# First attention's running sums as rounded high and low products, 384 columns at once

## The reference, cut to what matters

```python
z = jnp.einsum('bhqd,bhkd->bhqk', qb, kp) * scale
log_keep = jnp.where(mask, jax.nn.log_sigmoid(-z), 0.0)
later = lax.cumsum(log_keep, axis=3, reverse=True) - log_keep
a = jnp.where(mask, jnp.exp(jax.nn.log_sigmoid(z) + later), 0.0)
outs.append(jnp.einsum('bhqk,bhkd->bhqd', a, vp))
```

## Time and profile before

| | |
|---|---|
| three runs, median (lowest to highest) | 1855.86 us (1853.26 to 1858.29) |
| the profiled execution's own time | 1856.47 us |
| its span, first to last instruction | 1855.2 us |
| busy: PE, DVE, ACT, POOL | 92%, 64%, 41%, 22% of the span |
| first attention with its projections | about 24 to 131 us of the span |

### The profile page before, as it was taken

How to read it: one execution, slowest core, us unless ns; L and a number is a source line. 1 busy time by engine, 2 the same in 40 slices (tenths; PEclk the granted TensorE clock), 3 DMA queues, 4 the chain that set the end, 5 groups by cost and what they waited for, 6 DMA issues and landing times.

```text
span 1855.2 us, 23146 instructions
## 1 busy us (share of the span) xinstructions
PE 1704.7 (92%) x9262; PEld 1297.9 (70%) x9262; DVE 1187.9 (64%) x2130; ACT 753.1 (41%) x1323; POOL 402.9 (22%) x340
## 2 busy tenths in 40 slices
PE   8999999999999999999999999987888777878888
PEld 7979988977799888989989989873333333323333
DVE  5776645756476548854352666779677766677855
ACT  4655534344355436774353655443122121122211
POOL 0220000000000000003011000335645544545551
PEclk9999999999999999989999999999979988898899
DMA  6335554544445553423231325699999999999997
GB/s 253 135 120 213 183 187 176 182 167 160 164 173 191 189 181 137 171 83 107 77 113 46 111 78 184 256 393 419 423 421 421 423 420 422 422 421 421 422 421 299
DMA packets 62955, 453.85 MB, mean 245 GB/s; under 512 B 7000, under 2 KB 7128, under 8 KB 8448
## 3 DMA queue, kind: packets, MB, share of 16 engines
q0 software_dynamic: 37152, 268.45, 35.0%
q1 hardware_dynamic: 25040, 178.27, 27.0%
q10 hardware_dynamic: 656, 5.66, 0.9%
HBM read 451.15 MB, written 1.05 MB: 244 GB/s over the span
## 4 chain that ended last, share of the span: by engine, by line
PE 26%; DMA 14%; DVE 5%; ACT 2%; POOL 2%; issue 1%; DVEq 0%; ACTq 0%; POOLq 0%
DMA uv_rows<-expert_uv,index 14%; PE banks L2529 12%; PE banks L624 3%; PE banks L626 3%; PE banks L625 3%; DVE uv_rows L2715 3%; POOL uv_rows L2745 1%; PE banks L2303 1%; ACT diag L2594 1%; PE banks L1972 1%; PE banks L1961 0%; PE banks L2474 0%; PE banks L1954 0%; PE banks L2289 0%; POOL weights_lo L619 0%
## 5 line engine op out<-in xcount | busy, mean ns | idle before, releaser
L2529 PE MATMUL banks<-uv_rows,diag 128*128 128x512 f32 x1024 | 503.6, 654 | 116.9 <-ACT diag L2594 116.8
L610 DVE TENSOR_TENSOR weights_lo<-weights,weights_hi 128x1024 fp32r<-128x1024 f32 x325 | 397.2, 1263 | 256.2 <-ACT weights_hi L601 256.2
L2529 PEld LDWEIGHTS banks<-uv_rows,diag 128*128 128x128 f32 x1024 | 212.5, 211 | 406.7 <-issue 268.9
L601 ACT ACTIVATE weights_hi<-weights 128x1024 fp32r<-128x1024 f32 x328 | 329.2, 1052 | 356.1 <-PE banks L626 342.6
L624 PE MATMUL banks<-x_hi,weights_hi 128*128 128x256 f32 (+1 forms) x1472 | 427.6, 290 | 3.3 <-POOL weights_lo L619 1.2
L626 PE MATMUL banks<-x_hi,weights_lo 128*128 128x256 f32 (+1 forms) x1472 | 420.5, 286 | 0.0
L625 PE MATMUL banks<-x_lo,weights_hi 128*128 128x256 f32 (+1 forms) x1472 | 420.4, 286 | 0.0
L2715 DVE CUSTOM_DVE_ANT_0 uv_rows<-uv_rows,tokens 128x1024 f32<-128x1024 f32 x256 | 305.4, 1224 | 148.5 <-DMA uv_rows<-expert_uv,index 148.5
L2745 POOL DMA_INDIRECT uv_rows<-expert_uv,index x254 | 317.0, 1248 | 307.9 <-PE banks L2529 259.6
L624 PEld LDWEIGHTS banks<-x_hi,weights_hi 128*128 128x128 f32 x1472 | 282.0, 192 | 10.3 <-issue 3.0
L626 PEld LDWEIGHTS banks<-x_hi,weights_lo 128*128 128x128 f32 x1472 | 282.0, 192 | 0.0
(11 more groups left out here) (382 smaller groups left out, 2085.2 us busy)
## 6 DMA issues: line engine op xcount, KB each, us to landing
weights<-weights SPq DMA_DIRECT2D x164, 1024.0 KB, 4.8
uv_rows<-weights SPq DMA_DIRECT2D x4, 1024.0 KB, 7.7
uv_rows<-expert_uv,index POOLq DMA_INDIRECT x254, 17.5
sb_first<-constants_first ACTq DMA_DIRECT2D x1, 1920.0 KB, 8.6
sb_always<-constants_always ACTq DMA_DIRECT2D x1, 1627.5 KB, 6.8
sb_peer<-constants_peer ACTq DMA_DIRECT2D x1, 1544.0 KB, 7.8
h<-x SPq DMA_DIRECT2D x1, 1024.0 KB, 5.8
out<-h SPq DMA_DIRECT2D x4, 256.0 KB, 4.5
```

Source lines behind the costliest of these rows:

```text
L601: self.act.activation(self.w_hi[b % SLOTS][:, f], raw[:, f], ACT.Copy).then_inc(self.hi_made, 1)
L610: self.dve.tensor_tensor(self.w_lo[b % SLOTS][:, f], self.landing(b)[0][:, f], self.w_hi[b % SLOTS][:, f], ALU.subtract).then_inc(self.lo_ ...
L2529: mm = pe.matmul(self.bank(2 * t + half), self.diag[:, k, :], self.uv[ROW_BUFFER[n]][:, f], start=(u < NT and k == 0), stop=(u >= UNITS - ...
```

## The change

Before the sums, the masked softplus values are split: ScalarE copies them to float32r (`sb_sp_hi`, new `scalar_stick_hi`), VectorE subtracts for `sb_sp_lo` (new `vector_stick_lo`), for both heads of a pair in one instruction of 768 columns. The constants are copied once to float32r at the start (`sums_exact`). The sums become four float32r products per head instead of three plain ones: 384 columns of high, 384 of low, 128 of high, 128 of low. The semaphores `sb_log` and `shifted` now count twice per pair, and `sb_count` gives the count to wait for.

```diff
+    def sb_count(self, c, part):
+        return 4 * (c // 2) + 2 * part + c % 2 + 1
+
+    def scalar_stick_hi(self, c):
+        self.act.wait_ge(self.sb_kept, c + 1)
+        if c >= 2:
+            self.act.wait_ge(*self.attended("sums", "sb", c - 1))
+        self.act.activation(self.sb_parts[0][:, c % 2], self.sb_sp[:, c % 2], ACT.Copy).then_inc(self.sb_log, 1)
+
+    def vector_stick_lo(self, c):
+        self.dve.wait_ge(self.sb_log, self.sb_count(c, 1))
+        self.dve.tensor_tensor(self.sb_parts[1][:, c % 2], self.sb_sp[:, c % 2], self.sb_parts[0][:, c % 2],
+                               ALU.subtract).then_inc(self.attention["shifted"].sem, 1)
+
     def tensor_stick_sums(self, c):
         pe, b = self.pe, c % 2
-        pe.wait_ge(self.sb_kept, c + 1)
+        pe.wait_ge(*self.attended("shifted", "sb", self.sb_count(c, 1)))
         if c >= 2:
             pe.wait_ge(*self.attended("outputs", "sb", c - 1))
         for j in range(2):
             L = self.bank(2 * b + j)
-            pe.matmul(L[:, 0:S], self.C["from_here"][:, :], self.sb_sp[:, b, j, 0:S], start=True, stop=False)
-            pe.matmul(L[:, P:S], self.C["ones"][:, :], self.sb_sp[:, b, j, S:384], start=False, stop=True)
-            mm = pe.matmul(L[:, S:384], self.C["from_here"][:, :], self.sb_sp[:, b, j, S:384], start=True, stop=True)
+            hi, lo = (x[:, b, j] for x in self.sb_parts)
+            pe.matmul(L[:, 0:384], self.sums[:, 0, :], hi[:, 0:384], start=True, stop=False)
+            pe.matmul(L[:, 0:384], self.sums[:, 0, :], lo[:, 0:384], start=False, stop=False)
+            pe.matmul(L[:, P:S], self.sums[:, 1, :], hi[:, S:384], start=False, stop=False)
+            mm = pe.matmul(L[:, P:S], self.sums[:, 1, :], lo[:, S:384], start=False, stop=True)
@@ scalar_stick, at the start
         self.scalar_split(1)
+        for j, name in enumerate(("from_here", "ones")):
+            act.activation(self.sums[:, j, :], self.C[name][:, :], ACT.Copy)
@@ scalar_stick, in the loop
             self.scalar_stick_soft(c + 1)
+            self.scalar_stick_hi(c)
+            self.scalar_stick_hi(c + 1)
             self.scalar_split(qk + 2 * i + SLOTS)
@@ vector_stick, in the loop
             self.vector_stick_soft(c + 1)
+            self.vector_stick_lo(c)
+            self.vector_stick_lo(c + 1)
             self.vector_stick_diff(c)
             self.vector_split(qk + 2 * i + SLOTS)
```

More of the change, by code:

```diff
@@ L303, in memory @@
         self.sb_sp = self.place("sb_sp", [P, 2, 2, 384])
+        self.sb_parts = [self.place("sb_sp_" + n, [P, 2, 2, 384], F32R) for n in ("hi", "lo")]
+        self.sums = self.place("sums_exact", [P, 2, P], F32R)
         self.sb_a = self.place("sb_a", [P, 2, 2, 384])
@@ L498, in signals @@
         for n, signal in self.attention.items():
-            signal.plan("sb", SB_H // 2)
+            signal.plan("sb", SB_H if n == "shifted" else SB_H // 2)
             if n in ("scores", "values"):
@@ L1094, in vector_stick_neg @@
         if c >= 2:
-            dve.wait_ge(*self.attended("shifted", "sb", c - 1))
+            dve.wait_ge(*self.attended("shifted", "sb", self.sb_count(c - 2, 0)))
         dve.scalar_tensor_tensor(self.sb_e[:, c % 2], z, -1.0, z, ALU.mult, ALU.min).then_inc(self.attention["bounded"].sem, 1)
@@ L1099, in vector_stick_soft @@
         dve, b = self.dve, c % 2
-        dve.wait_ge(self.sb_log, c + 1)
+        dve.wait_ge(self.sb_log, self.sb_count(c, 0))
         if c >= 2:
-            dve.wait_ge(*self.attended("sums", "sb", c - 1))
+            dve.wait_ge(*self.attended("shifted", "sb", self.sb_count(c - 2, 1)))
         dve.scalar_tensor_tensor(self.sb_sp[:, b], self.sb_z[:, c % 3], 0.0, self.sb_e[:, b], ALU.max, ALU.add).then_inc(self.attention["shifted"].sem, 1)
@@ L1123, in gpsimd_stick @@
             for k in range(2):
-                pool.wait_ge(*self.attended("shifted", "sb", c + k + 1))
+                pool.wait_ge(*self.attended("shifted", "sb", self.sb_count(c + k, 0)))
                 own = self.own_tiles(self.sb_sp[:, k])
```

## The result

The changed kernel takes 1867.01 us (median of 4 runs, 1866.27 to 1869.81), the kernel before on the same chip 1854.91 (4 runs, 1853.26 to 1858.29): a ratio of 1.0065, 95% interval 1.0053 to 1.0077, so 12 us slower. I had forecast 1872 in 1862 to 1880.

The account below looks back on a forecast made before the run. TensorE was taken to bound the stretch. Turns cost 3.75 + 3.1 + 3.1 + 2.8 = 12.7 us at full clock; with half clock 14.6 to 19.1, taken as 16.5. 1855.86 + 16.5 gives 1872.4, said as 1872, range 1862 to 1880.

Parts of the forecast that it names:

- The saving: Sums on TensorE: a pair costs 1.15 us with the new products, saving 0.55 a pair, 4.4 over eight pairs.
- The wait in turn 1: Before the sums of pair 0, TensorE waits 3.96 us for high(0) on ScalarE, then low(0) on VectorE.
- Turns 2 and 3: The same wait recurs at 3.27 us; less 1.1 saved, plus 0.9 for the block, 3.1 us each.
- turn 4: Last turn of the attention: a wait of 2.0 us before pair 6's sums; values of pair 7 come 2.8 late.
- The block behind it: Next turn's block is late as VectorE and GpSimd contend for the SBUF port: 0.9 us more TensorE wait in turn 1.
- The sum at full clock: Attention, turns 1 to 4 without clock loss: 3.75 + 3.1 + 3.1 + 2.8 = 12.7 us.
- The clock: Half clock for 3 or 6 us behind the waits of turns 1 to 3 raises the loss to 14.6 or 19.1; 16.5 taken.
- the rule I drew from 27 of 28 waits: Expert stage: behind 27 of 28 waits of 2.48 us or more, the next 3 us run at clock 0.50 to 0.69.
- rival B: Attention: the clock also falls in turn 4 and 128-column products cost like plain ones; 24 us, 1880; chance 0.06.
- A: Attention: the clock stays up around the waits; 12.7 us, 1868.6; chance 0.14.
- C: Sums: TensorE does not wait for low(c); 4.4 us saved, 1851.5, if the delay vanished; chance 0.04.
- D: Later stages give the attention's waits back, so under 5.5 us remain; 1859; chance 0.06.

Follow-up runs that it names:

- saving_alone: Kernel before with the four new products per head, softplus written in the rounding type, zeros as low part, nothing split; 1852.36 us, ratio 0.9984.
- early: Changed kernel with the high and low steps moved to other places, mostly slots where ScalarE or VectorE waits; 1862.95 us, ratio 1.004.
- warm: Changed kernel with 32, 25, 25 and 16 extra TensorE products ahead of the waits before the sums of pairs 0, 2, 4, 6; 1868.28 us, ratio 1.0068.
- split_unused: Changed kernel with high and low parts made but unused, the sums plain and waiting only for the mask; 1868.1 us, ratio 1.0066.
- after_again: The changed kernel, unchanged, run and profiled once more; one run, 1873.27 us.
- block_first: Changed kernel with high(c+1) behind the block's split and low(c+1) behind the difference of c and the block's low part; 1876.73 us, ratio 1.012.

## Why the prediction was right, step by step

**The saving.** Predicted 1.15 a pair, 4.4 in all; measured 1.09, and 4.0 of work less in saving_alone. The 128-column products are at my two bounds in turn, 0.06 and 0.11.

**The wait in turn 1.** Each stamp was 0.2 to 0.3 late and the chain right: high(0) at 59.11 for 59.37, low(0) at 60.11 for 60.37, the sums at 61.12 for 61.35; 3.83 us for 3.96. Turns 2 and 3 have 2.99 for 3.27, turn 4 2.01 for 2.0. High parts are 0.83 to 0.84 for 0.85, low parts 0.95.

**The block behind it.** The mask held up by low(0) runs to 62.21, predicted 62.6, and the block's low part takes 3.45 beside a mask. The page "SBUF — State Buffer" of the Trainium skill, section "SBUF: two separate sides", on which I had leaned for this, is borne out: the mask takes 1.93 us beside a VectorE instruction with two SBUF inputs, 1.31 without, and low(1) in early 2.02 instead of 0.95. The second wait that I worked out for the block, 0.9 us a turn, was 0.45 where the clock was up (turn 3 of the profile after, and each turn of warm). What I had not seen is that this chain is about as long as the first by itself; split_unused showed it.

**The sum at full clock.** 12.7 predicted; 12.0 in warm, up to where its clock falls: 3.4, 2.9, 2.9 and 2.8 for 3.75, 3.1, 3.1 and 2.8. Turn 3 of the profile after, at clock 1.00, cost 2.8 for 3.1. Turn 4 adds the 2.8 that I gave it: 12.0 at the values of pair 4, 14.8 at those of pair 7. My own steps for turn 4 add up to 3.0 (123.7 for 120.72); that the 2.8 came out so exactly is luck in the last digit.

**The clock.** I took 16.5 less 12.7, 3.8 us. Against the 12.0 of warm it was 2.8 (14.8) and 4.6 (16.6) in the two profiles, so the size lies between them. By turn the profile after has 5.7, 3.6 and 2.8, and after_again 4.2, 4.8 and 5.0, for my 4.4 or 5.9, 3.7 or 5.2, 3.7 or 5.2: both lengths came, and once, in turn 3, none. So the rule I drew from 27 of 28 waits of the expert stage was too firm. It also left out turn 4, where I had the clock stay up and only rival B had it fall: it fell in both profiles (1.7 us of work each), as it did behind a wait of 1.73 us in warm and one of 1.85 in early. The turn cost 2.8 and 2.6 all the same. What I wrote ahead of warm, that turns 3 and 4 had no half clock, was wrong for turn 4. The Trainium skill, page "TensorE: Matmul & The Clock Gate", section "Why this matters for your kernels", says that gaps between bursts bring the clock down. The trace agrees behind five of the six waits of 2.99 us or more in two profiles, and disagrees behind one.

**The total.** 1872 predicted, 1867.0 measured; as a difference 16.5 predicted and 12.1 measured, with 14.8 and 16.6 in the attention of the two profiles. So the mechanism is right and the attention's size nearly so; as far as two profiles tell, the 4.4 us too many lie mostly outside the sum that I worked out. The attention's delay passes through, as I said, but the clock behind `lam` goes its own way: 16.69 to 21.28 us for the same work in ten profiles. That later stages are "unchanged" is true of their work and false of their time by up to 4.6 us. The profiled run of the four is a case of it: its 1866.27 is 11.4 over the median before, with 14.8 in the attention and the shortest of the ten stretches behind `lam`. The run of after_again is 19.3 over the median of its chip. The five runs of the changed kernel are thus 11.4 to 19.3 over, and the median of the first four is at the low end. What remains open is how much each timed run without a profile lost to the clock, and where.

**The rivals.** A, the clock stays up, is the nearest in time (1868.6 for 1867.0), and yet the profiles show 6.7 and 9.8 us of work lost to the clock: the time alone would have picked the wrong mechanism. C fell with the waits, D with the table, B's 24 us were reached by no run of this kernel, though the fall of the clock in turn 4 was part of B; block_first, at 22, shows what it takes.

**A version that beats before** was not found: early, the best with all of the computation, is 7.4 us behind it. The most that any run reached is saving_alone's 3 us, and only without the steps for the high and low parts. Room as such there is on VectorE: it is busy for 56.5 of the attention's 75.2 us before, and the eight low parts add 7.6. No order that was tried put them where they cost nothing; whether one exists is open.

## What to carry to other kernels

Before splitting an operand to make a product cheaper, compare what the bounding engine saves (here 0.55 us a pair) with what the split adds to the path of its input (0.83 + 0.95 us, behind whatever stands in the queue ahead of it), and place each new step in a slot in which its engine waits: that alone took the loss from 12 to 7 us. Look for a second chain of the same length before undoing the first: here taking away the wait that the profile names (split_unused) gained nothing in turn 1, 3.42 us either way, as a late block stood right behind it. And take the price of a wait as a range where the clock may fall behind it: the same wait in the same kernel left the clock at 1.00 once, and halved it for the next 5 us, 2.5 us of work, two other times.

## What the hardware did unexpectedly

Behind a wait of 2.99 us the granted clock of the next 5 us was 1.00, 0.66, 0.50 and 0.50. The length of the low stretch was not ordered by the length of the wait: that of 3.83 us had 0.50 behind it and that of 3.81 had 0.66. The clock also fell behind waits of 2.01, 1.83, 1.73 and one of the three of 1.85 us, and one of 3.63 us in the expert stage before (up to 1527.08) left the clock at 1.00. And a stretch of 113 or 114 products between two fixed points, with two waits of TensorE in it (2.07 to 2.09 and 1.55 us), took 16.69 us at clock 1.00, 18.15 to 18.22 in five profiles, 19.69 to 19.76 in three and 21.28 at 0.76, with nothing changed in it or ahead of it for 680 us. Two profiles of the changed kernel have spans of 1865.0 and 1872.0. A difference of a few us between single profiles of this kernel says nothing until it is followed to its stretch.
